# Constants multiplied on TensorE while it waits, blocks turned later, and a residual that starts two tiles apart

## The chip, the cores and the metric

The program runs on one core of one Trainium2 chip. The metric is the device time of one execution in microseconds (us). Engines are named as the profile names them: PE (TensorE matmul), PEld (its weight load), DVE (VectorE), ACT (ScalarE), POOL (GpSimd) and SP (the engine that issues nearly all DMAs).

## The reference, cut to what matters

Two blocks run one after the other on x (512 tokens of 1024 features, float32). The first has two hybrid layers:

```python
def hybrid_layer(x, c_act, positions, w_mod, b_mod, pre_gain, post_gain, w_in, sinks, ...):
    mod = c_act @ w_mod + b_mod
    shift, scale, gate = jnp.split(mod[:, None, :], 3, axis=-1)
    h = rms_norm(x, pre_gain) * (1.0 + scale) + shift
    proj = h @ w_in
    ...
    a_out = sliding_window_attention(aq, ak, av, sinks) * jax.nn.silu(ag)
    ...
    r_out = rms_norm(r).reshape(B, S, RET_W) * jax.nn.silu(rg)      # r: retention
    ...
    g_out = rms_norm(g, gla_norm_gain).reshape(B, S, GLA_W) * jax.nn.silu(gg)   # g: gated linear attention
    y = jnp.concatenate([a_out, r_out, g_out], axis=-1) @ w_out
    return x + gate * rms_norm(y, post_gain)
```

The second block has an even layer (x and a context ctx of 256 tokens) and an odd layer. Each of them is a mixer and then a feed-forward network:

```python
    mod = (s_c @ ada_w[l] + ada_b[l])[:, None, :]
    h = rms_norm_2(x, norm_g[l, 0]) * (1.0 + sc1) + sh1
    hc = rms_norm_2(xc, norm_g[l, 0]) * (1.0 + csc1) + csh1
    y, yc = mixer_even(h, hc, ...)        # l = 0; mixer_odd for l = 1
    x = x + g1 * rms_norm_2(y, norm_g[l, 1])
    h = rms_norm_2(x, norm_g[l, 2]) * (1.0 + sc2) + sh2
    x = x + g2 * rms_norm_2(swiglu(h, ffn_w_in[l], ffn_w_out[l]), norm_g[l, 3])
    # ctx goes the same way as x where the next layer needs it
```

Everything is float32. All large products are computed as three products of two float32 halves ("hi" and "lo").

## The kernel before

The program is a fixed list of phases, `schedule`. All engines go through it in the same order, and each phase has a method for every engine. Between most phases stands a barrier, `phase_end` (L241 to L245): each engine drains, adds one to `phase_done` and waits for all four. Phases for which `flows` (L247) is true have no barrier behind them: Linear and FeedForward before a residual, NormTransposed, MixTransposed, FirstWeights, and Residual itself.

The phases that matter here are:

- **NormTransposed** (L458): the normalised input, transposed, for the next product. ACT squares each row tile of 128 tokens (L503), POOL makes the factor (L508, L509), ACT a diagonal matrix of it (L513), and PE turns the tile by a matmul with that diagonal (L567), which leaves the turned blocks in banks of `ps`. The work then goes in groups; a group is one block of 128 features (kt, 0 to 7) of x (r=0, 512 tokens) or of ctx (r=1, 256 tokens). DVE applies scale and shift (L540, `h_full`), ACT rounds the high half (L528), and POOL subtracts to get the low half (L555). The tiles `ht_full`, `ht_high` and `ht_low` are also the names of the semaphores.
- **Linear** (L668) and **FeedForward** (L1317): products with streamed weights. A unit is 128x1024 values of weights: SP loads it (L274) to one of four slots of `w_raw`, ACT rounds `w_hi` (L283), POOL subtracts `w_lo` (L290) and PE multiplies three times (`matmul3`, L300 to L303). `ring_slot` (L261) lets SP load unit u only when unit u-4 has been read. The stream also has units of the modulation (c_act @ w_mod), which DVE sums up (L361).
- **Residual** (L808): the end of a Linear or FeedForward. DVE adds row tiles (L834) when the last of their output has left its bank and POOL has made their factor (L829, L830). The NormTransposed that follows is woven into its ACT and POOL parts (`norm.square`, `norm.factor`, `norm.diagonal`).
- **Attention** (L893), **Pieces** (L1228, small products and turns at L1257 and L1262), and **Work** (L1299): a phase of DVE, ACT and POOL work in which PE does nothing.

In a hybrid layer the order around the change is: Linear (w_in), Pieces, Attention, Work (retention decays), Pieces, Work (retention state), Pieces, Pieces, Work (log-decay), Work, Pieces, Pieces, GlaLevels, three Works, Pieces, Work (state of the gated linear attention), Pieces, Work (head norms, 16 us long), MixTransposed (L631), Linear (w_out), Residual.

In the layers with ctx the turned blocks are 16 and there are 8 banks, so PE turns some of them only when a bank is free. In the kernel before these late blocks are turned right behind the others, before the first weight unit:

```python
full = lambda kt, r: pe.wait_ge(ht_full.sem, self.f0 + 2 * kt + r + 1)
for tiles, kts, read in ((xt, (6,), [(0, 0)]), (xt, (7,), [(1, 0)]), (ct, (4, 5), [(0, 1), (1, 1)]), (ct, (6, 7), [(2, 0)])):
    full(*read[-1])
```

## Time and profile before

| | us |
|---|---|
| three runs: median (lowest to highest) | 2732.22 (2728.36 to 2737.06) |
| profiled execution, its own time | 2733.65 |
| span of the profile (first to last instruction) | 2731.8 |
| PE busy | 2374.6 (87%) |
| DVE, POOL, ACT busy | 1358.7, 1076.8, 852.2 |
| mean granted PE clock | 0.925 of full |

The profiled execution is 1.4 us above the median. The granted clock is a share of full speed: where it is 1.00 PE runs at 2.4 GHz, where it is 0.50 at 1.2 GHz.

### The profile page before, as it was taken

What the parts mean: (1) busy time and instruction counts of PE and PEld (TensorE: products, weight loads), DVE (VectorE), ACT (ScalarE), POOL (GpSimd) and SP (SyncE); (2) the same over time, 40 slices, a digit from 0 to 9 for tenths busy, and PEclk for the clock granted to TensorE, in tenths of its full rate; (3) what the DMA queues carried; (4) which work ended last, traced back from release to release, by engine and by line L of the source; (5) the groups of instructions that cost most, each with busy time, mean ns of one, the idle gap of its engine ahead of it and who ended that gap; (6) DMA issues with size and microseconds to landing.
All of it is one profiled execution on the core that took longest, in us unless ns stands there. A gap on an engine that the chain in (4) does not pass through costs nothing.

```text
span 2731.8 us, 32612 instructions
## 1 busy us (share of the span) xinstructions
PE 2374.6 (87%) x12690; PEld 1961.2 (72%) x12690; DVE 1358.7 (50%) x2043; ACT 852.2 (31%) x1624; POOL 1076.8 (39%) x793
## 2 busy tenths in 40 slices
PE   3888658988659878789979999999889899899998
PEld 3777437777437665456779898999778667788886
DVE  4875553795463966445944351223369774210012
ACT  2214113113204137365142121111321585322222
POOL 2433326333225324132264343343455243655554
PEclk9999769988769989799989999999999999999999
DMA  7540012540012420000523232323153000223332
GB/s 241 175 141 29 1 47 72 175 134 23 1 39 74 145 70 2 0 9 2 188 62 101 81 101 67 114 78 118 52 161 120 24 2 24 70 95 99 96 98 77
DMA packets 147730, 218.91 MB, mean 80 GB/s; under 512 B 18485, under 2 KB 71125, under 8 KB 147449
## 3 DMA queue, kind: packets, MB, share of 16 engines
q1 hardware_dynamic: 147576, 216.82, 25.0%
q8 instruction: 102, 1.67, 0.3%
q14 instruction: 52, 0.42, 0.0%
HBM read 214.69 MB, written 2.10 MB: 79 GB/s over the span
## 4 chain that ended last, share of the span: by engine, by line
PE 51%; DVE 3%; ACT 2%; issue 1%; POOL 1%; DMA 0%; ACTq 0%; DVEq 0%; POOLq 0%; SPq 0%
PE ps L301 13%; PE ps L302 13%; PE ps L303 13%; PE ps L975 4%; PE ps L1003 3%; PE ps L1025 1%; PE ps L1022 1%; PE ps L567 1%; PE ps L1262 1%; POOL h_transposed L555 1%; PE ps L388 1%; DVE x_tokens L834 0%; DVE mod_acc_aux L361 0%; ACT att_probs_lat L1061 0%; PE ps L1257 0%
## 5 line engine op out<-in xcount | busy, mean ns | idle before, releaser
L290 POOL TENSOR_TENSOR w_lo<-w_raw,w_hi 128x1024 fp32r<-128x1024 f32 (+3 forms) x252 | 591.5, 2348 | 1001.1 <-ACT w_hi L283 1001.0
L283 ACT ACTIVATE w_hi<-w_raw 128x1024 fp32r<-128x1024 f32 (+3 forms) x252 | 255.7, 1016 | 1176.8 <-PE ps L303 980.4
L301 PE MATMUL ps<-w_hi,h_transposed 128*128 128x512 f32 (+3 forms) x1088 | 419.3, 385 | 59.0 <-POOL w_lo L290 28.1
L302 PE MATMUL ps<-w_lo,h_transposed 128*128 128x512 f32 (+3 forms) x1088 | 410.4, 377 | 0.0
L303 PE MATMUL ps<-w_hi,h_transposed 128*128 128x512 f32 (+3 forms) x1088 | 410.1, 377 | 0.0
L301 PE MATMUL ps<-h_transposed,w_hi 128*128 128x384 f32 (+1 forms) x1056 | 374.6, 355 | 8.1 <-POOL h_transposed L555 6.5
L303 PE MATMUL ps<-h_transposed,w_lo 128*128 128x384 f32 (+1 forms) x1056 | 373.6, 354 | 0.0
L302 PE MATMUL ps<-h_transposed,w_hi 128*128 128x384 f32 (+1 forms) x1056 | 373.6, 354 | 0.0
L361 DVE SCALAR_TENSOR_TENSOR mod_acc_aux<-w_raw,c_act,mod_acc_aux 128x512 f32<-128x512 f32 x280 | 281.9, 1031 | 43.8 <-DMA w_raw<-in_w_mod_dram 20.5
L301 PEld LDWEIGHTS ps<-w_hi,h_transposed 128*128 128x128 f32 x1088 | 214.3, 197 | 105.1 <-POOL w_lo L290 32.8
L1454 DVE TENSOR_TENSOR ffn_full<-ps,ffn_silu 128x768 f32<-128x768 f32 (+1 forms) x44 | 34.2, 820 | 429.4 <-PE ps L303 429.4
L302 PEld LDWEIGHTS ps<-w_lo,h_transposed 128*128 128x128 f32 x1088 | 214.2, 197 | 34.7 <-issue 2.2
L303 PEld LDWEIGHTS ps<-w_hi,h_transposed 128*128 128x128 f32 x1088 | 213.9, 197 | 34.4
L301 PEld LDWEIGHTS ps<-h_transposed,w_hi 128*128 128x128 f32 x1056 | 199.3, 189 | 24.1 <-POOL h_transposed L555 8.4
L302 PEld LDWEIGHTS ps<-h_transposed,w_hi 128*128 128x128 f32 x1056 | 199.5, 189 | 13.7
L303 PEld LDWEIGHTS ps<-h_transposed,w_lo 128*128 128x128 f32 x1056 | 199.3, 189 | 13.9
L1098 DVE TENSOR_REDUCE attention_stats<-ps 128x1 f32<-128x768 f32 (+5 forms) x192 | 144.1, 774 | 65.0 <-PE ps L975 52.1
L301 PE MATMUL ps<-w_hi,ffn_hidden 128*128 128x512 f32 x440 | 174.2, 396 | 0.8 <-POOL ffn_hidden L1383 0.8
L302 PE MATMUL ps<-w_lo,ffn_hidden 128*128 128x512 f32 x440 | 174.6, 397 | 0.0
L303 PE MATMUL ps<-w_hi,ffn_hidden 128*128 128x512 f32 x440 | 173.1, 393 | 0.0
L1468 DVE TENSOR_TENSOR y_tokens<-y_tokens,ps 128x512 f32<-128x512 f32 x60 | 41.2, 687 | 166.9 <-PE ps L303 166.8
L361 DVE SCALAR_TENSOR_TENSOR mod_acc_gates<-w_raw,c_act,mod_acc_gates 128x512 f32<-128x512 f32 x84 | 104.6, 1272 | 15.4 <-DMA w_raw<-in_ada_w_dram 13.8
(310 smaller groups left out, 3560.8 us busy)
## 6 DMA issues: line engine op xcount, KB each, us to landing
w_raw<-in_ada_w_dram SPq DMA_DIRECT2D x96, 512.0 KB, 4.1
w_raw<-in_ffn_w_in_dram SPq DMA_DIRECT2D x88, 512.0 KB, 3.5
w_raw<-in_w_mod_dram SPq DMA_DIRECT2D x48, 512.0 KB, 4.6
w_raw<-in_ffn_w_out_dram SPq DMA_DIRECT2D x44, 512.0 KB, 3.6
w_raw<-in_w_in_dram SPq DMA_DIRECT2D x40, 512.0 KB, 4.2
w_raw<-in_w_out_dram SPq DMA_DIRECT2D x16, 512.0 KB, 4.9
w_raw<-in_od_w_in_dram SPq DMA_DIRECT2D x16, 512.0 KB, 4.0
mod_gain<-in_norm_g_dram SPq DMA_DIRECT2D x16, 256.0 KB, 4.0
```

Source lines behind the costliest of these rows:

```text
L283: act.activation(w_hi[:, i % 2, 0:k * n], w_raw[:, u % 4, 0:k * n], ACT.Copy).then_inc(w_hi_ready.sem, 1)
L290: pool.tensor_tensor(w_lo[:, i % 2, 0:k * n], w_raw[:, u % 4, 0:k * n], w_hi[:, i % 2, 0:k * n].bitcast(F32), ALU.subtract).then_inc(w_lo_ ...
L301: pe.matmul(acc, left[0], right[0], start=start, stop=False)
L302: pe.matmul(acc, left[0], right[1], start=False, stop=False)
L303: return pe.matmul(acc, left[1], right[0], start=False, stop=stop)
L361: ins = dve.scalar_tensor_tensor(out=self.acc[:, r], in0=w_raw[:, u % 4, j * HALF:(j + 1) * HALF], scalar=c_act[:, cond, 2 * q + j, c:c + ...
L388: ins = pe.matmul(ps[:, 6 + m % 2, 4 * i + j:4 * i + j + 1], self.acc[:, i, j * P:(j + 1) * P], ones[:, 0:1], start=True, stop=True)
L975: done.append(pe.matmul(sc[:, c:c + m], x["q"][i], x["keys"][i][k][0], start=True, stop=not masks))
L1003: ins = pe.transpose(ps[:, self.turn_bank(r), i * P:(i + 1) * P], self.probs[s % len(self.probs)][:, c:c + P], ident)
L1098: ins = dve.tensor_reduce(dst, src, AX, ALU.max, negate=True)
L1454: dve.tensor_tensor(view(full_t), ps[:, 4 + a * k:4 + (a + 1) * k, 0:w], view(silu_t), ALU.mult)\
L1468: ins = dve.tensor_tensor(y, y, ps[:, t, :], ALU.add)
```

## The change

- `keep_clock(pe, n)` multiplies the first 256 columns of the constants by the identity n times, into a bank that nobody reads. PE does this in Work phases (`clock=`: 6, 3, 6, 1, then 1, 1, 1, 7 and 33 in each hybrid layer, 8 and 12 in the even layer), in the first loops of six attention phases, and 8 times at the start of every NormTransposed that follows a Residual. It waits for nothing but what is ahead of it.
- In a layer with ctx the late blocks are turned by `turn_later`, called behind the first and second weight unit of a Linear (in FeedForward both behind the first); the banks are given out anew, and x's block 5 comes before ctx's block 4.
- The first weight unit starts with the products that need only the high halves (`begun`), and the waits for low halves are by group (`wait_part`).
- Both first weight units are now split on POOL before the groups (`prime`); where a Residual is ahead, the first is split before its tail.
- `Residual.steps` sets a new order: the second halves of two tiles leave their banks, then one row is added, and so on.

The diff, cut to its core; lines that only pass `clock` stand alone:

```diff
+        def keep_clock(pe, n, bank=7):
+
+            for _ in range(n):
+                pe.matmul(ps[:, bank, 0:2 * P], ident, con[:, 0:2 * P], start=True, stop=True)
...
+        def wait_part(pe, sig, source, kt, t):
+
+            first = source.h0 if sig is ht_high else source.g0
+            n = (kt + 1) * len(source.groups) // KT
+            if isinstance(source, NormTransposed):
+                n = source.index[kt, int(t >= XT)] + 1
+            pe.wait_ge(sig.sem, first + n)
...
+                if with_ctx:
+                    self.groups[9:11] = self.groups[10:8:-1]
...
+                self.later = [], []
                 if with_ctx:
-                    x_banks, ctx_banks = [4, 5, 7, 0, 2, 3, 4, 5], [6, 6, 1, 1, 6, 6, 7, 7]
+                    if self.ahead:
+                        x_banks, ctx_banks = [0, 1, 2, 3, 4, 5, 7, 7], [6, 6, 7, 7, 6, 6, 6, 6]
+                        self.later = [(1, (4, 5), (1, 1)), (0, (6,), (3, 1))], [(1, (6, 7), (5, 1)), (0, (7,), (6, 0))]
+                    else:
+                        x_banks, ctx_banks = [0, 2, 3, 4, 6, 7, 4, 6], [1, 1, 5, 5, 5, 5, 7, 7]
+                        self.later = [(1, (4, 5), (3, 1)), (0, (6,), (3, 0))], [(0, (7,), (4, 0)), (1, (6, 7), (5, 0))]
...
                             weights_high(act, *self.prime)
                         if step:
                             self.diagonal(act, step - 1)
-                weights_high(act, *self.prime)
+                    weights_high(act, *self.prime)
...
                     for t in range(self.T):
                         self.factor(pool, t)
+                    weights_low(pool, *self.prime)
                 weights_low(pool, *self.prime)
                 for g, (kt, r, tiles) in enumerate(self.groups):
-                    if g == 2 * len(self.groups) // KT:
-                        weights_low(pool, *self.prime)
...
             def tensor(self, pe):
+                if self.host is not None:
+                    self.host.bank_free(pe, 7)
+                    keep_clock(pe, 8)
...
-                full = lambda kt, r: pe.wait_ge(ht_full.sem, self.f0 + 2 * kt + r + 1)
-                for tiles, kts, read in ((xt, (6,), [(0, 0)]), (xt, (7,), [(1, 0)]), (ct, (4, 5), [(0, 1), (1, 1)]), (ct, (6, 7), [(2, 0)])):
-                    full(*read[-1])
+
+            def turn_later(self, pe, when):
+
+                for r, kts, (kt, read) in self.later[when]:
+                    pe.wait_ge(ht_full.sem, self.f0 + self.index[kt, read] + 1)
+                    tiles = range(XT, self.T) if r else range(XT)
                     for t in tiles:
                         self.turn(pe, t, kts, None, t == tiles[-1])
...
+                        begun = []
+                        if first == 0 and q == 0:
+                            begun = list(tiles[:4 if len(self.source.groups) == KT else 2])
+                            for i, t in enumerate(begun):
+                                wait_bank(pe, self.source, i)
+                                wait_part(pe, ht_high, self.source, 0, t)
+                                pe.matmul(ps[:, i, 0:n], HT[:, 0, 0, t * P:(t + 1) * P], w[0][:, 0, :], start=True, stop=False)
+                                pe.matmul(ps[:, i, 0:n], HT[:, 0, 0, t * P:(t + 1) * P], w[1][:, 0, :], start=False, stop=False)
+                            for i, t in enumerate(begun):
+                                wait_part(pe, ht_low, self.source, 0, t)
+                                pe.matmul(ps[:, i, 0:n], HT[:, 1, 0, t * P:(t + 1) * P], w[0][:, 0, :], start=False, stop=False)
...
+                        if first == 0 and q < 2 and isinstance(self.source, NormTransposed):
+                            self.source.turn_later(pe, q)
...
+            def steps(self):
+
+
+                k = -1 if isinstance(self.host, FeedForward) else 0
+                for t in range(self.T):
+                    yield "half", t
+                    if t % 2:
+                        yield "row", k
+                        k += 1
+                for t in range(k, self.T):
+                    yield "row", t
+
             def vector_tail(self, dve, second_half, gate=None):
                 gated = []
-                for step in range(self.T + 2):
-                    if step < self.T:
-                        second_half(step)
-                    if gate and 0 <= step - 1 < self.T:
-                        gated.append(dve_s.mark(gate(step - 1)))
-                    t = step - (2 if gate else 1)
-                    if 0 <= t < self.T:
+                for what, t in self.steps():
+                    if what == "half":
+                        second_half(t)
+                        continue
+                    if gate and t + 1 < self.T:
+                        gated.append(dve_s.mark(gate(t + 1)))
+                    if t >= 0:
                         if gate:
                             dve.wait_ge(dve_step.sem, gated[t])
                         self.add(dve, t)
 
             def scalar_tail(self, act, second_half):
                 norm = self.norm
-                for t in norm.ahead if norm else []:
-                    norm.square(act, t)
-                for step in range(self.T + 2):
-                    if step < self.T:
-                        self.square(act, 1, step, second_half(step))
-                    if norm and step == 0:
-                        for t in norm.ahead:
-                            norm.diagonal(act, t)
-                    if norm and step == self.T:
-                        weights_high(act, *norm.prime)
-                    if norm and 0 <= step - 1 < self.T:
-                        norm.square(act, step - 1)
-                    if norm and step >= 2:
-                        norm.diagonal(act, step - 2)
+                if norm:
+                    for t in norm.ahead:
+                        norm.square(act, t)
+                    weights_high(act, *norm.prime)
+                    for t in norm.ahead:
+                        norm.diagonal(act, t)
+                for what, t in self.steps():
+                    if what == "half":
+                        self.square(act, 1, t, second_half(t))
+                    elif norm and t >= 0:
+                        norm.square(act, t)
+                        if t:
+                            norm.diagonal(act, t - 1)
+                if norm:
+                    weights_high(act, *norm.prime)
+                    norm.diagonal(act, self.T - 1)
 
             def gpsimd(self, pool):
                 norm = self.norm
-                for t in norm.ahead if norm else []:
-                    norm.factor(pool, t)
-                for step in range(self.T + 1):
-                    if step < self.T:
-                        self.factor(pool, step)
-                    if norm and step:
-                        norm.factor(pool, step - 1)
+                if norm:
+                    for t in norm.ahead:
+                        norm.factor(pool, t)
+                    weights_low(pool, *norm.prime)
+                for what, t in self.steps():
+                    if what == "half":
+                        self.factor(pool, t)
+                    elif norm and t >= 0:
+                        norm.factor(pool, t)
...
+                    if loop < len(self.clock):
+                        keep_clock(pe, self.clock[loop], self.SUM_BANK)
...
-            def __init__(self, act=None, dve=None, pool=None, sp=None):
+            def __init__(self, act=None, dve=None, pool=None, sp=None, clock=0):
+                self.clock = clock
                 none = lambda eng: None
                 self.scalar, self.vector, self.gpsimd, self.sync = act or none, dve or none, pool or none, sp or none
 
             def tensor(self, pe):
-                pass
+                keep_clock(pe, self.clock)
...
+            schedule.append(Attention(steps, probs1, probs1_t, stats, neg_sinks, sinks, clock=(0, 0, 3)))
...
+            schedule.append(Work(dve=dve, pool=pool, clock=6))
...
+            schedule.append(Work(dve=dve, clock=3))
...
+            schedule.append(Work(act=act, dve=dve, clock=6))
...
+            schedule.append(Work(dve=lambda eng: eng.tensor_tensor(log_a, z_min, z_t, ALU.subtract), clock=1))
...
+            schedule.append(Work(dve=dve, act=act, pool=lambda eng: eng.memset(gla_s[:, 0], 0.0), clock=1))
...
+            schedule.append(Work(dve=dve, clock=7))
...
+            schedule.append(Work(dve=dve, pool=pool, sp=prelude_sp, clock=33))
...
+            schedule.append(Work(dve=dve, sp=sp, clock=8))
...
+            schedule.append(Work(dve=dve, clock=12))
...
+                schedule.append(Attention(steps, probsb, probsb_t, stats, clock=(3, 3)))
```

How that moves instructions, at three places. The first is POOL in the first NormTransposed of the program: `w_lo` is a weight unit, `h_transposed` the low half of a group. Before:

```order
L509 TENSOR_TENSOR rstd<-meansq,minus_half 128x1 [waits pool_step]
L290 TENSOR_TENSOR w_lo<-w_raw,w_hi 128x1024 [waits w_hi_ready]
L555 TENSOR_TENSOR h_transposed<-h_full,h_transposed 128x512 [waits ht_high,ht_full] x2
L290 TENSOR_TENSOR w_lo<-w_raw,w_hi 128x1024 [waits w_hi_ready]
L555 TENSOR_TENSOR h_transposed<-h_full,h_transposed 128x512 [waits ht_high,ht_full] x6
```

After:

```order
L530 TENSOR_SCALAR meansq<-sumsq 128x1 [waits squares_ready]
L531 TENSOR_TENSOR rstd<-meansq,minus_half 128x1 [waits pool_step]
L295 TENSOR_TENSOR w_lo<-w_raw,w_hi 128x1024 [waits w_hi_ready] x2
L576 TENSOR_TENSOR h_transposed<-h_full,h_transposed 128x512 [waits ht_high,ht_full] x8
L295 TENSOR_TENSOR w_lo<-w_raw,w_hi 128x1024 [waits w_hi_ready] x18
```

The second weight unit is no longer between the second and the third group; in the five NormTransposed behind a Residual the first unit stands ahead of the tail.

The second place is PE in the first hybrid layer, from the end of the retention scores to the log-decays of the gated linear attention. Before:

```order
L1262 MATMUL ps<-ret_q_t,ret_k_t 128x128
L1262 MATMUL ps<-ret_states,ret_qdecay_t 128x128 [waits phase_done]
...
L1262 MATMUL ps<-proj_one,ret_scores_t 128x64 x4
L1262 MATMUL ps<-gla_a_t,gla_gate_w 128x512 [waits phase_done]
L1257 MATMUL ps<-static_constants,gla_k_decayed_t 128x128 [waits phase_done]
L1257 MATMUL ps<-static_constants,gla_k_decayed_t 128x128 x3
L1262 MATMUL ps<-constants_one,gla_k_decayed 128x128 [waits phase_done]
```

After (L1320 and L1315 are what L1262 and L1257 were, L244 is `keep_clock`):

```order
L244 MATMUL ps<-static_constants 128x256 [waits phase_done]
L244 MATMUL ps<-static_constants 128x256 x2
L1320 MATMUL ps<-ret_states,ret_qdecay_t 128x128 [waits phase_done]
...
L1320 MATMUL ps<-gla_a_t,gla_gate_w 128x512 [waits phase_done]
L244 MATMUL ps<-static_constants 128x256 [waits phase_done]
L244 MATMUL ps<-static_constants 128x256 x5
L244 MATMUL ps<-static_constants 128x256 [waits phase_done]
L1315 MATMUL ps<-static_constants,gla_k_decayed_t 128x128 [waits phase_done]
```

Every constant product stands between two barriers, so it lies in the time of the Work phase and holds up the barrier behind it if it is longer.

The third place is PE in the Linear of the even layer, with ctx. Before, the last turned blocks and the first product:

```order
L567 MATMUL ps<-row_scales,x_tokens 128x128 [waits row_scales_ready] x3
L567 MATMUL ps<-row_scales,x_tokens 128x128 [waits row_scales_ready,ht_full]
L567 MATMUL ps<-row_scales,x_tokens 128x128
L567 MATMUL ps<-row_scales,x_tokens 128x128 [waits row_scales_ready]
...
L301 MATMUL ps<-w_hi,h_transposed 128x512 [waits ht_low,ht_full,w_lo_ready]
```

After, the end of the second weight unit and the start of the third:

```order
L308 MATMUL ps<-w_hi,h_transposed 128x512
L588 MATMUL ps<-row_scales,x_tokens 128x128 [waits row_scales_ready,ht_full]
L588 MATMUL ps<-row_scales,x_tokens 128x128
L588 MATMUL ps<-row_scales,x_tokens 128x128 [waits row_scales_ready]
L588 MATMUL ps<-row_scales,x_tokens 128x128
L588 MATMUL ps<-row_scales,x_tokens 128x128 [waits row_scales_ready,ht_full]
L588 MATMUL ps<-row_scales,x_tokens 128x128 [waits row_scales_ready] x3
L306 MATMUL ps<-w_hi,h_transposed 128x512 [waits ht_low,w_lo_ready]
```

Eight of the 16 late turns now stand behind the second unit (and eight behind the first), and the last groups of DVE, ACT and POOL come behind them.

## Rows read from the trace of the kernel before

**Rows 1.** The page: busy time of PE, and granted clock in 40 slices.

```profile
PE 2374.6 (87%) x12690; PEld 1961.2 (72%) x12690; DVE 1358.7 (50%) x2043; ACT 852.2 (31%) x1624; POOL 1076.8 (39%) x793
...
PEclk9999769988769989799989999999999999999999
```

**Rows 2.** The page: chain that ended last, shares of the span by engine.

```profile
PE 51%; DVE 3%; ACT 2%; issue 1%; POOL 1%; DMA 0%; ACTq 0%; DVEq 0%; POOLq 0%; SPq 0%
```

**Rows 3.** Windows: stretch, its length, busy of five engines, PEclk, DMA share, GB/s.

```profile
236.60:246.70 10.10, 9.37 (x46) 6.88 (x46) 5.38 (x23) 5.99 (x31) 4.22 (x13) 0.50 0.00 0
291.20:325.20 34.00, 17.89 (x62) 13.39 (x62) 11.71 (x14) 8.88 (x13) 9.17 (x6) 0.50 0.00 1
359.50:403.70 44.20, 21.77 (x83) 16.34 (x84) 20.01 (x38) 4.51 (x8) 11.52 (x7) 0.50 0.14 49
1124.10:1134.10 10.00, 7.74 (x33) 4.88 (x32) 6.93 (x15) 6.14 (x13) 0.00 (x0) 1.00 0.00 0
1134.30:1158.10 23.80, 19.27 (x37) 10.44 (x38) 5.92 (x11) 9.22 (x19) 5.33 (x3) 0.50 0.00 1
```

**Rows 4.** Timeline of PE, first hybrid layer: start, duration, instruction, idle before and releaser.

```profile
290.39 0.71 PE L1262 MATMUL ps<-ret_states,ret_qdecay_t 128*128 128x128 f32 x4 [2.62 <-DVEq L244]
...
300.79 2.07 PE L1262 MATMUL ps<-gla_a_t,gla_gate_w 16*128 16x512 f32 x2 [0.56 <-DVEq L244]
308.33 1.11 PE L1257 MATMUL ps<-static_constants,gla_k_decayed_t 128*128 128x128 f32 x4 [5.47 <-DVEq L244]
...
321.60 3.75 PE L2016 MATMUL ps<-gla_q_level,gla_k_level 128*128 128x512 f32 x4 [9.30 <-POOL gla_k_level L2005]
...
360.07 1.11 PE L1257 MATMUL ps<-static_constants,gla_k_decayed_t 128*128 128x128 f32 x4 [5.11 <-DVEq L244]
361.97 5.65 PE L1262 MATMUL ps<-proj_one,gla_k_decayed 64*128 64x256 f32 x16 [0.78 <-ACTq L244]
372.21 1.12 PE L1262 MATMUL ps<-gla_states,gla_q_decayed_t 128*64 128x256 f32 x4 [4.60 <-DVEq L244]
...
400.57 5.27 PE L631 MATMUL ps<-static_constants,proj_one 128*128 128x128 f32 x32 [16.48 <-DVEq L244]
```

**Rows 5.** Timeline of PE: the same kinds of matmul at either clock.

```profile
243.05 1.23 PE L975 MATMUL ps<-att_k_t,att_q_t 64*128 64x256 f32 x4
...
258.25 0.70 PE L975 MATMUL ps<-att_k_t,att_q_t 64*128 64x256 f32 x4
...
1111.88 1.03 PE L1262 MATMUL ps<-w_uq,latent_q_t 128*128 128x256 f32 x4
1112.74 1.02 PE L1262 MATMUL ps<-w_ukv,latent_kv_t 128*128 128x512 f32 x2
...
1121.09 2.07 PE L1262 MATMUL ps<-latent_kv_t,w_ukv 128*128 128x512 f32 x2 [6.46 <-DVEq L244]
```

**Rows 6.** Timeline of PE, DVE, SP and POOL: even Linear, first to third unit.

```profile
885.82 0.47 PE L301 MATMUL ps<-w_hi,h_transposed 128*128 128x512 f32 x1 [0.81 <-issue]
...
896.18 4.51 DVE L361 SCALAR_TENSOR_TENSOR mod_acc_aux<-w_raw,c_act,mod_bias 128x512 f32<-128x512 f32 x2
...
905.06 0.37 SPq L274 DMA_DIRECT2D w_raw<-in_ev_w_in_dram  x1
...
910.08 2.34 POOL L290 TENSOR_TENSOR w_lo<-w_raw,w_hi 128x1024 fp32r<-128x1024 f32 x1 [10.60 <-ACT w_hi L283]
...
912.47 0.79 PE L301 MATMUL ps<-w_hi,h_transposed 128*128 128x512 f32 x1 [6.79 <-POOL w_lo L290]
```

**Rows 7.** Timeline of POOL and PE: second hybrid layer, first low half and third unit.

```profile
463.05 2.52 POOL L555 TENSOR_TENSOR h_transposed<-h_full,h_transposed 128x512 fp32r<-128x512 f32 x2 [1.62 <-DVE h_full L540]
...
479.54 0.79 PE L301 MATMUL ps<-w_hi,h_transposed 128*128 128x512 f32 x1 [3.42 <-POOL w_lo L290]
```

**Rows 8.** Timeline, other boundaries: POOL at the program's start, DVE before the odd layer.

```profile
60.01 2.52 POOL L555 TENSOR_TENSOR h_transposed<-h_full,h_transposed 128x512 fp32r<-128x512 f32 x2 [4.55 <-DVE h_full L540]
...
1998.06 6.14 DVE L361 SCALAR_TENSOR_TENSOR mod_acc_aux<-w_raw,c_act,mod_bias 128x512 f32<-128x512 f32 x1
```

52 lines of the change are left out of this document (29 added, 23 removed).

## The prediction

> **What bounds the kernel now.** I read the page first: PE is busy 87% of the span, and the chain of what ended last is 51% PE and almost nothing else [rows 1, 2]; the rest of that chain is in its small lines, none of which is over 1% but on PE. So two things count: how long PE's work takes, and where PE stands still. The line of the granted clock [rows 1] says that PE is not always at 2.4 GHz: it has a 7 and a 6 in slices five and six, and again in eleven and twelve, which are the same phases of the two hybrid layers, and single dips later. The windows then show where [rows 3]: from 291.2 to 325.2 us and from 359.5 to 403.7 us the clock is 0.50 throughout, with PE busy in 17.9 of 34.0 us and 21.8 of 44.2 us. The timeline of PE shows why it is those stretches: they are short pieces of work between barriers, with gaps of 2.6, 5.5, 9.3, 5.1, 4.6 and 16.5 us, each ended by another engine (L244 is the barrier) [rows 4]. The other standstills are at the norms: PE waits for the third weight unit, 6.79 us in the even layer's Linear and 3.42 us in the second hybrid layer [rows 6, 7].
>
> **What low clock costs.** The same matmuls at either clock: four of 256 columns on 64 rows take 1.23 us at 0.50 and 0.70 at 1.00; two of 512 columns 2.07 and 1.02 [rows 5]. So work on the path shortens by 40 to 50% where the clock is full. Four instructions of 128x256 (two products of `keep_clock`'s form) advance PE by 1112.74 - 1111.88 = 0.86 us: 0.43 us each at full clock, 0.86 at half [rows 5].
>
> All gaps above lie on the path either way, since they are the time of DVE, ACT or POOL; what constants in them can give is the time of the work behind them. The Trainium skill, TensorE: Matmul & The Clock Gate, Terms, gives a price: throttled time times (1 - K/N). By it the stretch of 44.2 us would lose 22.1 us, which the row does not bear out: PE is busy in only 21.77 us of it, so that at most half of that can come back.
>
> **The constants, term by term** (change of the path in us, first and second hybrid layer).
> - Retention scores behind the Work of 6 products (2.6 us in a gap of about 3.9, so hidden): -1.2, -2.2, an estimate from a few us of work that begin at low clock.
> - Readout, 290.39 to 302.86: 12.47 us of short matmuls at 0.50 [rows 4], 7.5 to 7.9 at full: -5.0, -4.6. Its burst of 3 is 1.3 us in a gap of 2.62.
> - Log-decay pieces at 308.33 and behind: only some 4 us of PE work, and the 9.30 us gap ahead of 321.60 is inside GlaLevels, where no constants are: -1.5 each.
> - From 360.07 to 384.1: 1.1 + 5.65 + 11.9 = 18.6 us of work. If the three single products hold the clock over the 5.11 us gap, all of it gains, -9; if not, only the part behind the burst of 7 (3.0 us in a gap of 4.60), -3.8 net of the overrun of a burst that begins at half clock. Between the two: -6.1 each.
> - L631 at 400.57, 5.27 us: -1.6 each. Ahead of it the burst of 33 is 14.2 us in a gap of 16.48, hidden by 2.3 us. If x of the 33 run at half clock it takes 14.2 + 0.43x, so more than five of them would hold up the barrier.
>
> These make -15.4 and -16.0. The two attention starts have 0.50 for some 10 us with PE busy 9.37 [rows 3], and half of it lies on ACT's chain: -4 together. In the even layer: Work of 8, -1.2; attention, -3; Work of 12 ahead of 1121.09 (5.2 us at full clock in a gap of 6.46 [rows 5]), -1.5; the latent attentions, where 23.8 us stand at 0.50 [rows 3] with ACT releasing most steps, -3 and -2.5. The odd attention is at full clock already: 0. Sum of the clock: -31.4 - 4 - 11.2 = -46.6.
>
> **The norms, term by term.** POOL's queue is the slow one of a norm: a low half of 512 columns is 1.26 us (2.52 for two), a `w_lo` 2.34 [rows 6, 7]. Today the second unit's `w_lo` sits between the second and the third group. Moved ahead, it fills the 4.55 us in which POOL waits for `h_full` at 60.01 [rows 8]; its 2.4 us leave the chain that ends in the third unit: -2.4 there. In the second hybrid layer POOL waits only 1.62 us [rows 7], but now the first unit is split before the tail, and two gated halves leave at once; the low halves begin about 3 us sooner than 463.05: -4. The same at the even FFN (-4), at the odd Linear (-3.2) and at the odd FFN, where PE can now also begin with the high halves (-4.7). The last two are estimates by likeness, since the row of DVE at 1998.06, 6.14 us for one sum of modulations [rows 8], says that the third unit's slot is then held by DVE.
>
> The even Linear goes the other way. There the third unit's slot comes free only after eight modulation sums that DVE begins at 896.18, behind its last `h_full`; SP can issue the load at 905.06, POOL splits at 910.08, and PE starts at 912.47 [rows 6]. Two units of PE go from 885.82 to 905.68 (912.47 - 6.79). In the changed order the last blocks are turned behind the second unit, so DVE has its last `h_full` only when PE has done two units: PE's start comes some 5.5 us sooner (the 16 late turns and the DVE groups that they wait for are no longer ahead of it; an estimate), the second unit ends at about 899 to 900, the last `h_full` at 901 to 903, and then the eight sums, 8.9 us. Queued behind the sums are SP's load, ACT's rounding and POOL's split, and PE waits for those: about 918.4 against 912.47. +6, between +3 (the sums no longer meet POOL's low halves) and +7. At that length PE stands still some 15 us, which the earlier start has bought.
>
> The row 1998.06 is told by a page too: the Trainium skill, SBUF — State Buffer, Terms, says that DVE and GpSimd share a pair of ports, held by one for a full instruction. The trace agrees that DVE can wait long for POOL; by that rule all sums that meet POOL's low halves would be longer, and by the row's 6.14 us in place of about 1.1 a single meeting is worth 5 us. I leave it in the bounds.
>
> The last residual now has its rows later than today, with no norm behind it: +0.8. Sum of the norms: -2.4 - 4 + 6 - 4 - 3.2 - 4.7 + 0.8 = -11.5.
>
> Total -58.1. Against the profiled execution, 2733.65, that is 2675.6; the median of the runs is 1.4 lower. I say 2675.
>
> **The rivals.**
> - *The short matmuls do not hold the clock* (22%). For it: from 372.21 on PE works almost without a pause for 12 us and stays at 0.50, and so from 290.39 [rows 4, 3]; work that cannot raise the clock may not keep it. Against it: in attention matmuls of 64 and 256 columns run at full clock (258.25 [rows 5]). Then half of the clock's gain is left: 2733.65 - 23 - 11.5 = 2699.
> - *The late blocks trap DVE everywhere* (12%): the even FFN and the odd Linear gain nothing, and the even Linear loses 9: norms at about 0, 2687.
> - *More than I count* (12%): the three single products hold the clock, the latent attentions gain twice as much, and the even Linear loses nothing: 2655.
> - *The bursts run at half clock* (5%), the side of a slower kernel. A product is then 0.86 us: 33 of them are 28.4 in a gap of 16.48, +11.9 a layer; the bursts of 6, 6 and 7 overrun by 1.3, 0.7 and 2.3; so +32 in two layers, and +12 in the even layer (12 products in 6.46 us, and those in the attentions), with no gain: 2733.65 + 44 - 11.5 = 2766. It decides from the point above, where more than five of the 33 are slow. Against it: the wide matmuls at 1121.09 begin at half clock, and from 1124.1 on the clock is 1.00 [rows 5, 3], and the constants are wide matmuls without a wait. The page on the clock gate has the same rule, that activity releases the throttle, and a caveat that the clock was seen stuck low for 50 us and more; no row here shows such a thing with dense work.
> - *Nothing much* (4%): the gaps' clock falls anyway, and the norms trade wait for wait: 2725.
>
> My forecast as told has 45%, with a range of its own of 2662 to 2690. The range for 8 in 10 reaches to the halved clock gain above, with some of its spread, and to the larger gain below: 2650 to 2706. A difference of 0.3%, 8.2 us, is about what a measurement of this kernel can tell from no change. Faster: all but the last two cases and a little of the second, 0.91; within: 0.04; slower: 0.05.
>
> **What would show it.** In the profile after: the line of the clock has 9s in slices five, six, eleven and twelve; the windows from 290 to 303 us and from 360 to 403 us are mostly above 0.9; L1262's means fall; `keep_clock`'s matmuls have a mean that fits 0.43 us a product, and the barrier behind the head norms is released by DVE, not by PE. In the even Linear PE's wait for the third unit grows from 6.79 to near 15 us, and is near nothing at the two hybrid layers' third units. The prediction is wrong if the low clock remains in these stretches, if PE is what a barrier waits for, or if PE's gaps in the norms have only moved.

## The result, and the profile after

| | us |
|---|---|
| before, four runs: median (lowest to highest) | 2734.64 (2728.36 to 2737.12) |
| after, four runs: median (lowest to highest) | 2696.95 (2691.66 to 2699.14) |
| ratio after to before, 95% interval | 0.9864 [0.9848, 0.9879] |
| profiled execution after, its span | 2691.66, 2689.9 |
| forecast, and its range | 2675.0, 2650.0 to 2706.0 |

The kernel became 37.7 us faster by the medians, 1.4%. The forecast had 58.1 us; the measured time lies in its range, and 22 us above it. The span of the profiled execution fell by 41.9 us (2731.8 to 2689.9); this execution is 5 us faster than the median of its kind.

The page of the changed kernel: PE's busy time, the granted clock in 40 slices and the chain that ended last, to be read beside [rows 1, 2].

```profile
PE 2417.7 (90%) x13114; PEld 1997.4 (74%) x13114; DVE 1354.3 (50%) x2043; ACT 852.6 (32%) x1624; POOL 1082.6 (40%) x793
...
PEclk9999889999799899999899999999999999999999
...
PE 49%; DVE 4%; POOL 2%; ACT 2%; issue 1%; DMA 1%; ACTq 0%; DVEq 0%; POOLq 0%
```

PE is busy 43 us longer than before, since 424 instructions of constants take 110.4 us, and the other work of PE takes 67 us less. The slices of the hybrid layers have two 8s and one 7 where there were 7 and 6 twice. Part of the low clock is still there, and the windows show where; columns as in [rows 3]:

```profile
349.80:363.30 13.50, 11.80 (x32) 8.72 (x32) 6.28 (x12) 0.60 (x1) 0.00 (x0) 0.50 0.00 0
363.40:390.00 26.60, 24.55 (x143) 20.19 (x142) 13.00 (x26) 3.47 (x6) 11.08 (x7) 1.00 0.24 81
680.00:694.00 14.00, 11.87 (x89) 10.21 (x87) 6.56 (x18) 1.18 (x3) 0.00 (x0) 1.00 0.00 1
762.00:788.00 26.00, 23.84 (x141) 19.90 (x139) 13.49 (x27) 3.77 (x7) 11.38 (x7) 1.00 0.30 102
```

And the timeline of PE in the same places (L244 is `keep_clock`, two instructions a product), first hybrid layer and then the second:

```profile
293.50 6.09 PE L244 MATMUL ps<-static_constants 128*128 128x256 f32 x14 [1.33 <-DVEq L249]
...
347.66 2.47 PE L244 MATMUL ps<-static_constants 128*128 128x256 f32 x6 [2.67 <-DVEq L249]
352.11 5.65 PE L1320 MATMUL ps<-proj_one,gla_k_decayed 64*128 64x256 f32 x16 [0.78 <-ACTq L249]
358.59 5.62 PE L244 MATMUL ps<-static_constants 128*128 128x256 f32 x14 [0.83 <-POOLq L249]
...
371.40 14.51 PE L244 MATMUL ps<-static_constants 128*128 128x256 f32 x66 [0.56 <-ACTq L249]
387.32 3.71 PE L658 MATMUL ps<-static_constants,proj_one 128*128 128x128 f32 x32 [1.40 <-DVEq L249]
...
754.02 2.96 PE L1320 MATMUL ps<-proj_one,gla_k_decayed 64*128 64x256 f32 x16 [0.78 <-ACTq L249]
758.04 3.29 PE L244 MATMUL ps<-static_constants 128*128 128x256 f32 x14 [1.05 <-POOLq L249]
```

The burst of 33 is 14.51 us, 0.44 us a product, and ends 1.40 us before the barrier lets PE go on; L631 of before is L658 now, and takes 3.71 us in place of 5.27 [rows 4]. The burst of 7 takes 5.62 us in the first layer, nearly all of it at 0.50, and 3.29 us at 1.00 in the second: the three single products did not hold the clock in the first layer and held it in the second (the same 16 matmul instructions behind them take 5.65 and 2.96 us).

The even layer's Linear, engines PE, DVE, SP and POOL, to be read beside [rows 6]:

```profile
847.51 0.47 PE L792 MATMUL ps<-w_hi,h_transposed 128*128 128x512 f32 x1 [0.54 <-ACT h_transposed L550]
...
858.86 1.71 DVE L562 TENSOR_SCALAR h_full<-ps,mod_columns 128x256 f32<-128x256 f32 x3 [4.55 <-PE ps L588]
868.82 0.54 DVE L562 TENSOR_SCALAR h_full<-ps,mod_columns 128x256 f32<-128x256 f32 x1 [8.25 <-PE ps L588]
...
870.89 2.41 DVE L366 SCALAR_TENSOR_TENSOR mod_acc_aux<-w_raw,c_act,mod_bias 128x512 f32<-128x512 f32 x2
...
878.02 0.37 SPq L279 DMA_DIRECT2D w_raw<-in_ev_w_in_dram  x1
...
882.67 2.66 POOL L295 TENSOR_TENSOR w_lo<-w_raw,w_hi 128x1024 fp32r<-128x1024 f32 x1 [8.78 <-ACT w_hi L288]
...
885.39 0.80 PE L306 MATMUL ps<-w_hi,h_transposed 128*128 128x512 f32 x1 [15.71 <-POOL w_lo L295]
```

DVE stands 4.55 and 8.25 us for the late blocks, and then sums; SP, ACT and POOL follow, and PE stands 15.71 us for the third unit. From the first product of the norm's consumer to the third unit it was 26.65 us before (885.82 to 912.47) and is 37.88 now.

To find where the time went I took PE's start or end at the same step in each trace and subtracted that of before. In us; negative is sooner. The steps are the end of the hybrid layers' last Pieces (start of the output product at 825.27), the end of the even Linear (986.62), the start of the even output product (1286.73), the end of the first products of the even feed-forward network (1499.50), the end of the odd Linear (2128.91), the start of the odd output product (2294.79) and the end of PE's work (2721.65). The labels are those of the experiments below.

| trace | 825 | 987 | 1287 | 1500 | 2129 | 2295 | 2722 |
|---|---|---|---|---|---|---|---|
| after | -36.6 | -27.3 | -44.3 | -38.1 | -41.8 | -41.0 | -42.2 |
| c_after (the same kernel) | -34.9 | -27.1 | -41.3 | -34.8 | -37.0 | -36.9 | -41.0 |
| e1_no_constants | -3.2 | +6.6 | +8.8 | +12.7 | +9.0 | +11.1 | +7.5 |
| e2_constants_only | -29.2 | -30.1 | -42.1 | -42.5 | -42.3 | -42.4 | -44.0 |
| e3_blocks_early | -32.8 | -33.4 | -49.5 | -44.9 | -51.2 | -51.6 | -54.0 |
| c_blocks_early (the same kernel) | -36.3 | -35.2 | -51.5 | -49.8 | -53.8 | -53.6 | -57.7 |
| e5_sums_ahead | -39.2 | -39.1 | -53.0 | -44.4 | -50.4 | -50.0 | -51.4 |

Two traces of the same kernel differ by up to 5 us at a step. The first column shows that this is not all: up to there after, c_after, e3, c_blocks_early, e5 and e9_one_sum_first (experiment 7, -29.4) run the same instructions, and they lie between -29.4 and -39.2. So a difference of a few us between two single traces shows nothing by itself; it is read where both traces of a kernel agree or where a wait in the timeline explains it.

### The profile page after: what moved, and what is told of

It reads as the page before. It is cut to its first block, busy times and chain, and to the rows that moved or that the text cites. A ratio compares the mean times of both kernels' runs of the same rounds, so it can differ in the third digit from the quotient of the medians.

```text
span 2689.9 us, 33492 instructions
## 1 busy us (share of the span) xinstructions
PE 2417.7 (90%) x13114; PEld 1997.4 (74%) x13114; DVE 1354.3 (50%) x2043; ACT 852.6 (32%) x1624; POOL 1082.6 (40%) x793
## 4 chain that ended last, share of the span: by engine, by line
PE 49%; DVE 4%; POOL 2%; ACT 2%; issue 1%; DMA 1%; ACTq 0%; DVEq 0%; POOLq 0%
PE ps L306 13%; PE ps L307 13%; PE ps L308 13%; PE ps L1031 4%; PE ps L1059 2%; PE ps L1081 1%; PE ps L1078 1%; DVE mod_acc_aux L366 1%; PE ps L1320 1%; PE ps L393 1%; PE ps L588 1%; DVE proj_odd L1277 0%; DVE rope_tmp_odd L1274 0%; POOL w_lo L295 0%; POOL h_transposed L576 0%
## 5 line engine op out<-in xcount | busy, mean ns | idle before, releaser
L306 PE MATMUL ps<-w_hi,h_transposed 128*128 128x512 f32 (+3 forms) x1060 | 405.8, 383 | 63.7 <-POOL w_lo L295 43.7
L307 PE MATMUL ps<-w_lo,h_transposed 128*128 128x512 f32 (+3 forms) x1060 | 397.2, 375 | 0.0
L308 PE MATMUL ps<-w_hi,h_transposed 128*128 128x512 f32 (+3 forms) x1060 | 396.8, 374 | 0.0
L306 PEld LDWEIGHTS ps<-w_hi,h_transposed 128*128 128x128 f32 x1060 | 207.4, 196 | 104.1 <-POOL w_lo L295 47.6
L307 PEld LDWEIGHTS ps<-w_lo,h_transposed 128*128 128x128 f32 x1060 | 208.0, 196 | 33.7 <-issue 2.2
L308 PEld LDWEIGHTS ps<-w_hi,h_transposed 128*128 128x128 f32 x1060 | 207.2, 195 | 32.9
L244 PE MATMUL ps<-static_constants 128*128 128x256 f32 x424 | 110.4, 414 | 18.1 <-DVEq L249 8.0
```

The source lines that it names most:

```text
L244: pe.matmul(ps[:, bank, 0:2 * P], ident, con[:, 0:2 * P], start=True, stop=True)
L306: pe.matmul(acc, left[0], right[0], start=start, stop=False)
L307: pe.matmul(acc, left[0], right[1], start=False, stop=False)
L308: return pe.matmul(acc, left[1], right[0], start=False, stop=stop)
```

## The experiments

**1. The change without the constants, and the constants alone.** The first has everything but `keep_clock`'s matmuls:

```diff
-            for _ in range(n):
+            for _ in range(0):
                 pe.matmul(ps[:, bank, 0:2 * P], ident, con[:, 0:2 * P], start=True, stop=True)
```

> The changed kernel with keep_clock issuing nothing; everything else of the change stays. Theory, read from the two traces (PE's steps shifted by about -40 us in the stretches with constants and by about -1 us over all norms together): this kernel is the old one within 3 us, 2731 to 2736, ratio to before 0.999 to 1.001. Rival, the sum as predicted (norms -11.5): 2722, ratio 0.996. A second rival, that reordering costs by itself and the constants hide it: 2740 or more.

Measured: 2741.32 us (12 runs), before 2735.95 (17 runs), ratio 1.002 [1.0008, 1.0032]. It is slower than before, by 5.4 us, beyond the 3 us of the theory and a little beyond the second rival's 2740: the reordering costs by itself, and the forecast 2722 for it is out.

The second is the kernel before with `keep_clock` and all its call places:

```diff
+        def keep_clock(pe, n, bank=7):
+            for _ in range(n):
+                pe.matmul(ps[:, bank, 0:2 * P], ident, con[:, 0:2 * P], start=True, stop=True)
...
-            schedule.append(Work(dve=dve, pool=pool, sp=prelude_sp))
+            schedule.append(Work(dve=dve, pool=pool, sp=prelude_sp, clock=33))
```

> The kernel before with keep_clock at every place where the changed kernel has it, and nothing else of the change. Theory: the whole of the gain is here, 2692 to 2698, ratio to before 0.985 to 0.987, and it does not differ from the changed kernel by more than 3 us. Rival, the terms as predicted (constants -46.6): 2687, and the rest of the change costs 9 us. Second rival, the parts need each other (a norm that starts sooner keeps the clock): 2705 or more.

Measured: 2691.16 us (4 runs), the same before, ratio 0.9836 [0.9818, 0.9855]. That is -44.8 us for the constants alone, against -46.6 in my sum. It is just below the theory's 2692, and 5.8 us faster than the whole change (2696.95), where the theory allowed 3. Within the spread the two halves add up: -44.8 + 5.4 = -39.4, and the whole change is -37.7 (-38.7 in its second measurement, below). So no part needs the other, and the kernel would have been faster with the constants only.

**2. The late blocks.** The changed kernel with the late blocks turned ahead of the first weight unit again, and with them the banks and the order of two groups as they were before:

```diff
-                    self.groups[9:11] = self.groups[10:8:-1]
...
-                        x_banks, ctx_banks = [0, 1, 2, 3, 4, 5, 7, 7], [6, 6, 7, 7, 6, 6, 6, 6]
-                        self.later = [(1, (4, 5), (1, 1)), (0, (6,), (3, 1))], [(1, (6, 7), (5, 1)), (0, (7,), (6, 0))]
...
+                    x_banks, ctx_banks = [4, 5, 7, 0, 2, 3, 4, 5], [6, 6, 1, 1, 6, 6, 7, 7]
...
+                for tiles, kts, read in ((xt, (6,), [(0, 0)]), (xt, (7,), [(1, 0)]), (ct, (4, 5), [(0, 1), (1, 1)]), (ct, (6, 7), [(2, 0)])):
+                    full(*read[-1])
```

> The changed kernel with the late blocks of the layers with ctx turned where the kernel before turned them, ahead of the first weight unit, with the old banks and order of groups; the rest stays. Theory, late blocks hold DVE behind PE's weight units, and so the modulation sums, and so the loads that wait for their slots: at the third unit of the even Linear PE's wait falls from 15.7 to 7 to 9 us, and the even feed-forward network gets back some 3 us; the kernel is 6 to 12 us faster than the changed one, 2685 to 2691. Rival, the early start of the first units is worth the same as the late loads cost: 2695 to 2700. Second rival, the early start is worth more: 2703 or more.

Measured: 2675.44 us (5 runs), ratio 0.9779 [0.976, 0.9797], and once more as a neighbour of later runs:

> The kernel with blocks turned early once more, as the neighbour of the other three on this chip. Theory: 2672 to 2680, ratio to before 0.977 to 0.981.

Measured: 2678.42 us (4 runs), ratio 0.9792 [0.9769, 0.9815]. To know that this is no matter of the chip, the changed kernel ran again too:

> The changed kernel once more, unchanged, so that the others of this group stand beside it on the same chip. Theory: 2690 to 2700, ratio to before 0.984 to 0.988; the kernel with blocks turned early, 2675.4 on another chip, is then truly some 20 us faster. Rival, that the 20 us are the chip: 2680 or less.

Measured: 2695.97 us (5 runs), before 2734.64 (9 runs), ratio 0.9864 [0.9839, 0.9889]. So the late turning, with its banks and its order, costs 0.7% to 0.85%, 17.5 to 21.5 us by the medians, more than the 6 to 12 that I expected, and the intervals do not touch. The rivals, that the early start of the first units is worth what the late loads cost, or more, are out. PE at the third unit of the even Linear:

```profile
854.00 0.47 PE L790 MATMUL ps<-w_hi,h_transposed 128*128 128x512 f32 x1 [0.81 <-issue]
...
878.32 0.79 PE L306 MATMUL ps<-w_hi,h_transposed 128*128 128x512 f32 x1 [6.73 <-POOL w_lo L295]
```

The wait is 6.73 us again in place of 15.71. In the table the even Linear (825 to 987) costs +9.3 and +7.8 with late blocks, -0.6 and +1.1 without, and the stretch of the odd Linear (1500 to 2129) gains 3.7 and 2.2 with them, 6.3 and 4.0 without. The stretch from 1287 to 1500 costs +6.2 and +6.5 with them, and still +4.6 and +1.7 without.

**3. Is it the sums behind the late blocks?** The changed kernel, late blocks as they are, but DVE sums in its waits for them:

```diff
             def vector(self, dve):
+                ahead = {10: 1, 13: 2} if linear else {10: 2}
                 for g, (kt, r, tiles) in enumerate(self.groups):
+                    for _ in range(ahead.get(g, 0) if units else 0):
+                        job, q = units.pop(0)
+                        job.sum(dve, q)
```

> The changed kernel, late blocks as they are, but in the three norms with ctx DVE does two to three units of the modulation sums that the next phase owes in the times in which it waits for the late blocks (one ahead of ctx's block 4 and two ahead of ctx's block 6 in a Linear, two ahead of ctx's block 4 in the feed-forward network). Theory, late blocks cost time only because the sums, and with them the loads that need their slots, come behind them: PE's wait for the third unit of the even Linear falls from 15.7 to about 6 us, and the kernel gains 10 to 18 us on the changed one, 2680 to 2686. Rival, the loss of the late blocks lies elsewhere (in the groups' own order, in the smaller starts of PE): within 4 us of the changed kernel.

Measured: 2684.87 us (5 runs), ratio 0.9824 [0.98, 0.9849], beside 2695.97 for the changed kernel on the same chip: -11.1 us. The timeline of DVE, SP and PE:

```profile
851.71 2.10 DVE L366 SCALAR_TENSOR_TENSOR mod_acc_aux<-w_raw,c_act,mod_bias 128x512 f32<-128x512 f32 x2
...
858.86 7.19 DVE L366 SCALAR_TENSOR_TENSOR mod_acc_aux<-w_raw,c_act,mod_acc_aux 128x512 f32<-128x512 f32 x8
...
863.18 0.37 SPq L279 DMA_DIRECT2D w_raw<-in_ev_w_in_dram  x1
...
874.17 0.80 PE L306 MATMUL ps<-w_hi,h_transposed 128*128 128x512 f32 x1 [7.03 <-POOL w_lo L295]
```

SP's load is issued at 863.18, before the last blocks are turned, and PE's wait is 7.03 us; the even Linear costs +0.1 in the table. So at this place the theory holds: late blocks cost time because the sums, and the load that waits for their slot, stood behind them. It is not all of it: the kernel is still 6 to 9 us behind the one with early blocks. In the even feed-forward network the edit made it worse. From the middle of the output product (1355.78 in the trace before) to the end of that network's first products (1499.50) PE loses 3.2 and 3.3 us in the two traces of the changed kernel, 6.0 with the sums ahead, and 1.4 and 0.3 with early blocks. PE waits there for low halves of the late blocks and not for a weight unit, in the changed kernel and with the sums ahead:

```profile
1371.16 0.45 PE L306 MATMUL ps<-h_transposed,w_hi 128*128 128x384 f32 x1 [1.71 <-POOL h_transposed L576]
```

```profile
1359.76 0.44 PE L306 MATMUL ps<-h_transposed,w_hi 128*128 128x384 f32 x1 [1.73 <-POOL h_transposed L588]
...
1362.57 0.69 PE L306 MATMUL ps<-h_transposed,w_hi 128*128 128x384 f32 x1 [2.02 <-POOL h_transposed L588]
```

In the odd Linear PE's wait stays at 7.57 us. There it is POOL's order. In the changed kernel and in this one the third unit's `w_lo` stands behind the low halves of the late groups, in the changed kernel at:

```profile
1965.36 0.80 PE L306 MATMUL ps<-w_hi,h_transposed 128*128 128x512 f32 x1 [7.51 <-POOL w_lo L295]
```

With early blocks the same wait is 2.52 us, in both traces, and the next unit waits again, 2.87 and 4.28 us. That it is POOL's order is read from the order of its instructions and the releaser, and was not tried by itself.

**4. The longest burst.** The changed kernel with `clock=0` in place of 33:

```diff
-            schedule.append(Work(dve=dve, pool=pool, sp=prelude_sp, clock=33))
+            schedule.append(Work(dve=dve, pool=pool, sp=prelude_sp, clock=0))
```

> The changed kernel without the 33 products beside the head norms in both hybrid layers (14.2 us of PE each). Theory, a burst gives only the time of the work right behind it: L631 (5.27 us before, 3.8 after) and the first matmuls of the Linear fall back to the low clock, +1.5 to +2.5 us a layer, 3 to 5 us in all: 2700. Rival, the burst is longer than the head norms and holds up the barrier, so it is faster without: 2693. Second rival, long bursts are what keeps the clock up later too: +10 us or more, 2707.

Measured: 2703.26 us (5 runs, 2693.24 to 2706.11), ratio 0.9875 [0.9855, 0.9896], against 0.9864 for the changed kernel. Its PE at the place:

```profile
387.95 5.31 PE L658 MATMUL ps<-static_constants,proj_one 128*128 128x128 f32 x32 [16.48 <-DVEq L249]
```

The wait for DVE is the 16.48 us of before, so the burst lengthened nothing (the first rival is out), and L658 is at 5.31 us again. The median is 6.3 to 7.3 us above the changed kernel, the interval of the ratio overlaps with it: between the theory (3 to 5) and more than that the runs do not decide. In the traces the stretch from the last short matmuls (381.07 and 800.39 before) to the output product gains 2.7 and 2.9 us with the burst and 1.3 and 0.3 without, 4.0 us in all. The two profiled executions are 14.4 us apart. 5.1 of that lie between 406 and 643 us, where the run without the burst gains nothing and the changed kernel 4.9, but two kernels with the burst (e9_one_sum_first and e10_both of experiment 7) only 1.5 and 1.8; another 5.1 lie behind 825 us, where both run the same instructions. So what the burst is worth beyond the 4.0 is not shown.

**5. Shorter bursts.** Blocks early, and the bursts that begin at low clock cut:

```diff
-            schedule.append(Work(dve=dve, pool=pool, clock=6))
+            schedule.append(Work(dve=dve, pool=pool, clock=3))
...
-            schedule.append(Work(act=act, dve=dve, clock=6))
+            schedule.append(Work(act=act, dve=dve, clock=4))
...
-            schedule.append(Work(dve=dve, clock=7))
+            schedule.append(Work(dve=dve, clock=4))
```

> The kernel with blocks turned early, with the bursts of 6, 6 and 7 of the two hybrid layers cut to 3, 4 and 4. Theory, in the changed kernel these bursts begin at the low clock and take 0.8 us a product there, and hold up their barriers by 2.7, 1.3 and 2.1 us; cut, they end in their gaps and the clock rises as well: -4 to -8 us on 2675.4, 2668 to 2672. Rival, shorter bursts no longer raise the clock for the short matmuls behind them: +5 to +12 us, 2681 to 2687.

Measured: 2678.11 us (5 runs), ratio 0.9797 [0.9774, 0.982]; the neighbours of the same kernel with long bursts are 0.9779 and 0.9792. Neither the theory's gain nor the rival's loss: no difference that these runs can tell. The burst behind the state product is short now:

```profile
358.94 3.35 PE L244 MATMUL ps<-static_constants 128*128 128x256 f32 x7 [0.83 <-POOLq L249]
```

and the short matmuls behind it still gain: in the first layer PE is 9.7 us ahead at 321.60 and 14.4 us at the end of the short matmuls (384.10), where the changed kernel had 10.0 and 13.3. PE's pause around this burst is 4.69 us (4.60 before, 6.53 in the changed kernel), and around the burst of the log-decay work 5.61 (5.47 before, 7.50 in the changed kernel). So the local overruns are gone, but the whole is no faster.

**6. The residual's order.** Blocks early, with the tails of before:

```diff
-                for what, t in self.steps():
+                for step in range(self.T + 2):
+                    if step < self.T:
+                        second_half(step)
```

> The kernel with blocks turned early (2675.4 us), with the residual's tail in the order of the kernel before (one half tile, one row, in turn); the weight unit stays ahead of it. Theory, two halves at once let POOL and ACT reach the last diagonal sooner by about 1.5 us at each of five norms: without it +5 to +9 us, 2681 to 2684. Rival, the order moves nothing, since the last half tile sets the last row: within 3 us of 2675.4.

Measured: 2680.51 us (5 runs), ratio 0.9804 [0.9779, 0.9829]; +2 to +5 us on the two measurements of the kernel with the new order, with overlapping intervals. The runs do not decide between the theory and the rival.

**7. Two things in the even layer.** Before, after and with early blocks the even output product's third unit starts 21.2 us after DVE's first low half (1285.63 to 1306.86 before), so that an earlier first unit only waits longer:

```diff
-                        if first == 0 and q == 0:
+                        if first == 0 and q == 0 and isinstance(self.source, NormTransposed):
```

> Blocks turned early, and the first weight unit starts with the high halves only where a norm is its source, not behind a MixTransposed. Theory, in the even output product the third unit is set by DVE's sums (21.2 us from DVE's first low half to PE's third unit in both traces), so an earlier first unit only lengthens PE's wait there from 1.8 to 4.6 us, and the clock falls behind it for 3.4 us, which costs 1.7; without it -1 to -3 us on the neighbour. Rival, the wait and the fall come from elsewhere: within 1 us or slower by 1 to 2 us.

Measured: 2679.7 us (4 runs), ratio 0.9799 [0.9775, 0.9823], neighbour 2678.42. PE there with early blocks, and in this kernel:

```profile
1258.40 0.80 PE L306 MATMUL ps<-w_hi,h_transposed 128*128 128x512 f32 x1 [4.61 <-POOL w_lo L295]
```

```profile
1257.61 0.50 PE L306 MATMUL ps<-w_hi,h_transposed 128*128 128x512 f32 x1 [1.82 <-POOL w_lo L295]
```

The wait fell as the theory says, and the matmul behind it is at full clock (0.50 in place of 0.80 us). Over the output product (1286.73 to 1355.78 before) PE loses nothing in this trace, but 1.5 us in that of both edits together (below), which has the same edit; with the early start of the high halves it loses 3.0 and 3.2 us in the two traces of the changed kernel, 3.2 and 1.4 with early blocks. The kernel's time does not show it: +1.3 us on the neighbour, which is what the rival said.

The other edit lets DVE sum one unit ahead of the first group of the even layer's norms:

```diff
             def vector(self, dve):
+                ahead = {0: int(not ffn)} if linear else {0: 1}
```

> Blocks turned early, and in the even layer's Linear and feed-forward network DVE does one unit of the modulation sums in its wait of 4.1 and 2.8 us ahead of the first group. Theory, the load for the third unit of the even Linear is released by the second unit of sums, which now comes 3 us sooner: -2 to -5 us on the neighbour. Rival, the sum meets POOL's small steps of the last row factors and delays the whole norm by as much: +1 to +4 us.

Measured: 2675.81 us (4 runs), ratio 0.9784 [0.9763, 0.9805]. PE's wait at the third unit of the even Linear went from 6.76 us in the neighbour to 3.09:

```profile
878.11 0.80 PE L306 MATMUL ps<-w_hi,h_transposed 128*128 128x512 f32 x1 [3.09 <-POOL w_lo L295]
```

and the median by -2.6 us: as the theory says, but inside the spread. Both edits together:

> The two edits before this one together. Theory: their sum, -3 to -8 us on the neighbour, about 2670. Rival, one of the two takes the other's gain: that of the better one alone.

Measured: 2672.95 us (5 runs), ratio 0.9775 [0.9754, 0.9796]: the lowest of all, 5.5 us below its neighbour, and 0.9% below the changed kernel (0.9864 [0.9839, 0.9889]). Against that neighbour the intervals overlap, so the sum that the theory adds up and the rival's better one alone (-2.6) are not told apart; against the changed kernel the intervals do not overlap.

## Why the prediction was right, and where its size was off

**The number.** The measured 2696.95 lies in the stated range, 2650 to 2706, but outside the 2662 to 2690 that I gave the forecast as told. The upper end of the range was drawn for another mechanism, the rival in which half of the clock's gain is missing (2699). That the time lay inside is in part luck: the clock gave what was forecast, and the norms, forecast at -11.5, cost 5.4.

**The constants: right in sum, nearly right in their parts.** Forecast -46.6, measured alone -44.8. By the table the hybrid layers give -29.2 (forecast -35.4 with the attention starts), the even layer's attention part -12.0 (-11.2), the rest -2.8 (0). The largest piece of the shortfall is where I had said that I chose between two ends, -9 and -3.8: behind GlaLevels the three single products hold the clock only sometimes. Both ends came true. From 360.07 to the end of the short matmuls at 384.10 PE gains 3.4 us in the first layer after, where the clock was not held, and 8.3 in the second, where it was; c_after, the same kernel, gains 3.4 in each. Of the 24 places in the twelve traces with these products the clock was held in 7. With the constants alone it was held in neither layer (-7.8 in all, forecast -12.2).

The bursts that begin at half clock overran: PE's pause at the log-decay work grew from 5.47 to 7.50 us in the first layer (6.09 us for 7 products) and to 6.53 in the second, the one at the retention decays from 3.89 to 5.17 in the second, and the one at the burst of 7 from 4.60 to 6.53 in the first. I had priced the first two kinds as hidden, at full clock, and only the last as an overrun; in the rival on half clock I gave the burst of 7 an overrun of 2.3, though 7 times 0.86 in a gap of 4.60 is 1.4. The rival in which bursts run at half clock thus happened at single places, and never at the burst of 33 (14.51 us in every trace that has it), where it would have decided.

**Do the short matmuls hold the clock?** Their rival (22%, 2699) gave nearly the measured time, and for the wrong reason: behind a burst these matmuls ran at full clock in both layers. The readout took 5.57 us (284.73 to 290.30) where it took 9.84 (290.39 to 300.23), the last ones 6.54 (364.30 to 370.84) where they took 11.89. But each time they were over within 7 us, and the clock fell 1.4 us behind the readout, while the next product (290.86 to 292.16) ran:

```profile
284.70:291.60 6.90, 6.31 (x50) 5.73 (x50) 0.85 (x2) 0.77 (x2) 0.00 (x0) 1.00 0.01 2
291.70:298.40 6.70, 5.37 (x13) 3.87 (x12) 2.16 (x5) 3.86 (x5) 0.00 (x0) 0.50 0.01 1
```

In both layers of all twelve traces with constants it fell 1.3 to 3.4 us behind the readout, and in the run without the burst of 33 it fell at 374.2, 2.7 us behind the last short matmul, in an idle stretch. That the short matmuls alone would have held it for longer is not shown; they did not need to.

**The norms: the term that failed.** The prediction put them at -11.5, "-2.4 - 4 + 6 - 4 - 3.2 - 4.7 + 0.8". Measured without constants they are +5.4 by the medians, +7.5 in the trace. Place by place in that one trace: the two hybrid norms -3.2 (forecast -6.4); the even Linear +9.8 (+6, range +3 to +7); the even output product +2.0 (0) and the even feed-forward norm +2.0 (-4); the odd Linear's stretch -3.7 (-3.2); the odd output product to the end -3.6 (-3.9); and 2.2 and 2.1 us lost in the even and odd attention, for which I had no term and which are no larger than what two traces of one kernel differ by.

Two steps failed. In the even Linear the mechanism was told rightly, and experiment 3 confirms it, but it was worth 8 to 10 us, not 6. The step that was mis-sized is PE's earlier start, "some 5.5 us". Counted from the lead of 36.5 us with which PE comes into this norm, the first product starts 1.8 us sooner (847.51 against 885.82), the last `h_full` of DVE ends near 907.5 on the scale of before and not at 901 to 903, and the third unit starts 9.4 us later than before. DVE's sums up to the load took 7.1 us in place of the 8.9 that I had queued. The wait of "some 15 us" came out (15.71), but my own times, 899 to 900 for the end of the second unit and 918.4 for the third, leave more than that.

The other is the sentence that the even feed-forward network gains "the same" 4 us. It lost 3.2 and 3.3 us in the traces of the changed kernel. Its late blocks are turned behind the first unit, and DVE waits for them:

```profile
1364.80 1.71 DVE L562 TENSOR_SCALAR h_full<-ps,mod_columns 128x256 f32<-128x256 f32 x3 [8.12 <-PE ps L588]
```

This looks like the trap of the even Linear, but it is not the sums: with sums put ahead of the late blocks the place became dearer (6.0), and what PE waits for is POOL's low halves of the late blocks (experiment 3). The late blocks are a part of the loss only, for with early blocks the place still costs 1.4 and 0.3 us, and over all seven traces with early blocks it lies between -1.1 and +1.4, where I had -4; why the gain did not come stays open. The output product ahead of it, for which I had no term, loses 1.3 to 3.2 us in the traces with constants and the early start of the high halves, and 0 and 1.5 in the two without that start (experiment 7). The rival "the late blocks trap DVE everywhere" (12%, 2687) had the size of the even Linear (9); the odd Linear did gain, and the feed-forward network lost by another wait.

With early blocks the rest of the norm changes is worth 2691.16 - 2675.44 = 15.7 us beside the constants, and 12.7 by the second measurement. The forecast time, 2675, is that of the kernel without late turning (2675.44 and 2678.42), but by chance: my sum has +6 for the late turning in it, and without that it says -17.5 for the norms and 2669.

**What was checked against the signs named.** The clock's line improved, but to 8s and a 7, not 9s: in the first layer the clock was still 0.50 from 349.8 to 363.3. `keep_clock` is 0.44 us a product at full clock. The head norms' barrier is released by DVE; the barriers behind the bursts named above wait for PE. PE's wait at the even Linear is 15.71. At the second hybrid layer's third unit a wait for POOL's `w_lo` remains, where I expected next to nothing:

```profile
463.59 0.50 PE L306 MATMUL ps<-w_hi,h_transposed 128*128 128x512 f32 x1 [3.07 <-POOL w_lo L295]
```

It was 3.42 us before [rows 7]: that split still stands behind the eight low halves on POOL, which all moved forward with it.

## What to carry to other kernels

Idle time of TensorE between short phases costs twice, once as idle and once in the clock of what follows, and a few wide matmuls without a wait give the second part back: here 1.6% with no other change. A burst should be sized for the case that it starts at the low clock, unless its gap is long enough for either; here such overruns were 1.1 to 2.0 us at a place, and cutting them did not show in the kernel's time (experiment 5).

Before an engine's work is moved behind another's, look at what stands behind it in program order on the waiting engine: here the matmuls moved were 16 small ones, and what they held up was a queue of sums, the DMA whose slot the sums free, and the split of that load. If they must be late, the waiting engine's next work can be pulled ahead into the wait, which gave back about half of the loss here (11.1 of 17.5 to 21.5 us), in one place of three.

## What the runs showed of the hardware that I had not expected

The clock's state behind the three single products differs from layer to layer in one execution (the same 16 matmul instructions take 5.65 us in the first layer and 2.96 in the second; 2.96 or 2.97 in 7 of 24 places), and two profiled executions of the same kernel are apart by up to 5 us at the same step. So effects of 2 us at one place are seen in a trace's row and do not show in the kernel's median.

Short matmuls of 64 to 256 columns ran 12 us almost without a pause at 1.2 GHz before, and stayed there [rows 4]; behind a burst the same matmuls run at 2.4 GHz for the 5.57 and 6.54 us that they then take.

One modulation sum of DVE took 6.17 us in the odd Linear of the kernel with early blocks and 6.14 before [rows 8], while POOL went from one low half to the next and on to a `w_lo` without a pause; the three sums behind it took 2.33 us together in both, and the same first sum took 0.78 us in the changed kernel (1959.51). The Trainium skill, SBUF — State Buffer, Terms, has a pair of ports that DVE and GpSimd take for a whole instruction; the trace agrees. It fits a DVE that does not get its turn between two of POOL's instructions when these are back to back: the sum ends 0.56 us after POOL's `w_lo` (1949.86 to 1952.19), and POOL began four instructions while it ran. This is a reading of the timeline and was not tried by itself.
